# State-space chunks of a hybrid decoder trunk: sums between the rounds, read in their bank, lags shared with ACT, the skip term on GpSimd

## The chip, the cores and the metric

The kernel runs on one core of a Trainium2 chip. Its time is the device time of one execution in microseconds (us); three executions were timed before the change. One further execution was recorded by the profiler, and every row below is from it. TensorE (PE in the rows, PEld its weight loads) multiplies, VectorE is DVE, ScalarE is ACT, GpSimd is POOL and SyncE is SP; SP issues transfers.

## The reference

The program is a decoder trunk of two layers over 1024 tokens of width 1024. The change touches one part of the second layer's mixer, a diagonal state-space layer: 512 channels in 32 groups of 16, with 64 complex states a group.

```
ug = u.reshape(b, s, S5_GROUPS, S5_GROUP_CH)
bu_re = einsum('bsgc,gpc->bsgp', ug, bb_re)         # bu_im likewise
_, _, xr, xi = associative_scan(combine, (ar, ai, bu_re, bu_im), axis=1)   # x_t = a x_(t-1) + bu_t
y = einsum('bsgp,gcp->bsgc', xr, c_re) - einsum('bsgp,gcp->bsgc', xi, c_im)
y = y.reshape(b, s, S5_CH) + d_skip * u32
hg = gelu(y)
```

## The kernel before, in words

The sequence is cut into 128 chunks of `STEP` = 8 tokens, so that one matmul operand holds the 8 x 16 values of a chunk of one group on 128 partitions. Three things are needed. `q.into` turns a chunk into what it adds to the states (powers of the state matrix times B). `lags` holds for each of the 8 distances inside a chunk the 16x16 matrix C A^n B of a group; it is written on 16 partitions and then spread by eight transfers over the 128 partitions of `q.within`, each shifted by one token. And a scan over chunks carries the states along. `d_skip` enters as a diagonal added to the matrices of distance 0.

`s5_chunks` is one stage: it starts and ends with a barrier of all engines, and each engine's instructions run in the order in which they are written, held back only by semaphores. `NB` is 8 (one unit n is four groups), `P` 128, and a quarter k (0 to 3) is eight groups, thus units 2k and 2k+1. Every PSUM tile (`pa`, `pk`, `pb`, `pz`) has two banks, used in turn by even and odd n.

- TensorE: eight rounds; in each it transposes a unit of the powers (L2368, `pa`) and multiplies it with C (L2376, `pk`). ACT copies `pa` into `q.into` (L2414, tile `h` in the rows), VectorE copies `pk` into `lags` (L2432).
- VectorE then adds the skip term (L2436, made by L2427 from `d`), and SP issues the eight transfers (L2474, `h<-lags`). TensorE's first `outputs` waits for all of them (`spread`).
- `turn_u(n)` (L2324) transposes u, ACT copies it into `ut` (L2404), which lies in the memory of the powers (`bpow` in the rows; u itself is `gdn_t`). `sum_up(n)` (L2334) multiplies `q.into` with it into `pb`.
- VectorE, once a quarter: four copies of sums out of `pb` (L2448, L2449), a complex product with cosines and sines (L2110 to L2115 of `complex_times`: four products and two sums), two scans (L2457, L2458), and a second complex product. Then `scanned` is raised.
- `outputs(n)` (L2351 to L2353) adds three matmuls for each of four groups into `pk`, ACT applies gelu (L2410, into `s_t`), `turn_y` (L2361) transposes back, VectorE's `out` (L2440) writes y, in the memory of u.
- `keep_busy` (L131) issues matmuls whose results nobody reads.

In the order before, TensorE runs all rounds, then `turn_u` and `sum_up` from quarter to quarter, with the sums of quarter k+1 ahead of or beside the outputs of quarter k-1. Each `sum_up` of a later quarter waits for VectorE's copies (`s_copied`), each output for `scanned`. The next stage's work, `s5_glu` with its weights' transfers, starts behind the barrier.

Of the kernel before, what the change touches and what calls it, by code (L numbers as in the profile page):

```python
# [11 lines left out]
ALU = mybir.AluOpType  # L12
# [3 lines left out]
P = 128  # L16
# [2275 lines left out]
def s5_chunks(nc, c, t, j, q, bpow, u, scratch):  # L2292
# [3 lines left out]

    y = output_of(u)
    QP, NB = PAIRS // 4, S5_GROUPS // 4
    ut = bpow[:].rearrange("p a t s -> p (a t) s")
    with ExitStack() as ctx:  # L2300
# [8 lines left out]
                 "summed", "s_copied", "scanned", "y_made", "y_copied", "y_turned", "y_out", "vec_steps")  # L2309
        with stage(nc, *names) as (block, (b_turned, b_copied, multiplied, k_copied, spread, d_in, skip_ready, skipped, u_turned, u_copied,  # L2310
                                           summed, s_copied, scanned, y_made, y_copied, y_turned, y_out, vs)):
            def group(n, a):
                return 8 * (n // 2) + 2 * a + n % 2

            @block.tensor
            def _(pe):
                def turn_u(n):
                    if n == 0:
                        pe.wait_ge(b_copied, NB)
                        pe.wait_ge(multiplied, NB)  # L2320
                    if n >= 2:
                        pe.wait_ge(u_copied, n - 1)
                    for a in range(4):
                        last = pe.transpose(pa[:, n % 2, a * P:(a + 1) * P], u[:, 4 * n + a, :, :].rearrange("p s c -> p (s c)"), c.ident[:])  # L2324
                    last.then_inc(u_turned, 1)

                def sum_up(n):
                    pe.wait_ge(u_copied, n + 1)
                    if n >= 2:
                        pe.wait_ge(s_copied, n - 1)  # L2330
# [8 lines left out]
                def outputs(n):  # L2339
                    if n == 0:  # L2340
                        pe.wait_ge(spread, 16 * STEP)
                        pe.wait_ge(k_copied, NB)
# [21 lines left out]
                for n in range(NB):  # L2364
                    if n >= 2:
                        pe.wait_ge(b_copied, n - 1)
                    for a in range(4):
                        last = pe.transpose(pa[:, n % 2, a * P:(a + 1) * P], bpow[:, a % 2, 2 * n + a // 2, :], c.ident[:])  # L2368
                    last.then_inc(b_turned, 1)
                    if n >= 2:  # L2370
                        pe.wait_ge(k_copied, n - 1)
                    for a in range(4):
                        g = group(n, a)
                        half = slice((g % 2) * S5_STATE, (g % 2 + 1) * S5_STATE)
                        for part, cc in ((0, q.c_re), (1, q.c_nim)):
                            last = pe.matmul(pk[0:S5_GROUP, n % 2, a * P:(a + 1) * P],  # L2376
                                             bpow[half, part, g // 2, (STEP - 1) * S5_GROUP:STEP * S5_GROUP],
                                             cc[half, g // 2, 0:STEP, :], start=(part == 0), stop=(part == 1))
                    last.then_inc(multiplied, 1)
                for k in range(6):  # L2380
                    if k < 4:
                        turn_u(2 * k)
                        turn_u(2 * k + 1)
                    if k == 2:
                        keep_busy(pe, c, pz[:, 0], 24)
                    if 1 <= k <= 4:
                        sum_up(2 * k - 2)
                        sum_up(2 * k - 1)
                    if k >= 3:
                        outputs(2 * k - 6)  # L2390
                        outputs(2 * k - 5)
# [9 lines left out]
            def _(act):  # L2401
                def u_copy(n):
                    act.wait_ge(u_turned, n + 1)
                    act.activation(ut[:, 4 * n:4 * n + 4, :].rearrange("p g c -> p (g c)"), pa[:, n % 2, :], ACT.Copy).then_inc(u_copied, 1)  # L2404
# [16 lines left out]
            def _(dve):  # L2421
                step = Steps(dve, vs)
                for a in range(2):
                    dve.memset(x_re[:, a, :, 0:1], 0.0)
                    dve.memset(x_im[:, a, :, 0:1], 0.0)
                dve.wait_ge(d_in, 16)
                dve.tensor_tensor(skip, d[:].unsqueeze(2).to_broadcast([S5_GROUP, S5_GROUPS, S5_GROUP]),  # L2427
                                  c.ident[0:S5_GROUP, 0:S5_GROUP].unsqueeze(1).to_broadcast([S5_GROUP, S5_GROUPS, S5_GROUP]),
                                  ALU.mult).then_inc(skip_ready, 1)
                for n in range(NB):  # L2430
                    dve.wait_ge(multiplied, n + 1)
                    dve.tensor_copy(lags[:, 8 * (n // 2) + n % 2:8 * (n // 2) + 8:2],  # L2432
                                    pk[0:S5_GROUP, n % 2, :].rearrange("p (g s) -> p g s", g=4)).then_inc(k_copied, 1)
                dve.wait_ge(skip_ready, 1)
# [815 lines left out]
```

## Time and profile before

| | us |
|---|---|
| median of three timed executions | 3115.54 (3115.08 to 3117.53) |
| the profiled execution's own time | 3113.26 |
| its span, first to last instruction | 3111.7 |
| TensorE busy | 2926.2 (94%), mean granted clock 0.975 |
| VectorE, ACT, GpSimd busy | 1129.9 (36%), 668.1 (21%), 238.4 (8%) |

Three executions differ by 2.5 us. The shares are means over a program whose stages have different limits, so they say little of one stage of some 87 us. In it the reader looks at which engine waits for which, row by row. The granted clock is a share of TensorE's full speed: 1.00 is 2.4 GHz, 0.50 is 1.2 GHz.

### The profile page before, as it was taken

How to read it: one execution, taken by the hardware profiler on the slowest of the kernel's cores; microseconds unless marked ns; L12 is line 12 of the kernel's file. 1: busy time of each engine (PE TensorE's matmuls, PEld its weight loads, DVE VectorE, ACT ScalarE, POOL GpSimd, SP SyncE). 2: the span in 40 equal slices, each digit the busy share in tenths (PEclk: the TensorE clock that was granted, in tenths of full speed). 3: DMA queues.
4: the chain of work that ended last, by engine and by line, in shares of the span. 5: the costliest groups of instructions: out<-in, count | busy, mean ns of one | idle time of the engine just before them, and what ended most of it. 6: DMA issues, size and time to landing. Idle time of an engine off the chain costs nothing. (4 is left out here: it accounts for less than half of the span.)

```text
span 3111.7 us, 33248 instructions
## 1 busy us (share of the span) xinstructions
PE 2926.2 (94%) x12773; PEld 1588.0 (51%) x12774; DVE 1129.9 (36%) x2472; ACT 668.1 (21%) x1278; POOL 238.4 (8%) x344
## 2 busy tenths in 40 slices
PE   7999999999999999988989999878999999999798
PEld 5544555555544444434467744477555444444343
DVE  2585355534300000005464635565563000000152
ACT  3310355531110101003321224322211101010130
POOL 0000000001000000002000000144110000000110
PEclk9999999999999999999999999889999999999899
DMA  4000791031599999966020110000416999999631
GB/s 159 27 27 0 285 407 65 1 118 57 186 422 410 413 412 413 395 274 230 34 65 1 29 56 27 1 2 29 158 57 263 410 419 413 411 413 400 264 136 41
DMA packets 138551, 617.26 MB, mean 198 GB/s; under 512 B 25188, under 2 KB 31748, under 8 KB 121992
## 3 DMA queue, kind: packets, MB, share of 16 engines
q1 hardware_dynamic: 111848, 529.08, 43.0%
q0 software_dynamic: 23168, 82.85, 6.9%
q10 hardware_dynamic: 3376, 3.19, 0.3%
q8 instruction: 103, 1.69, 0.2%
q14 instruction: 56, 0.46, 0.0%
HBM read 508.00 MB, written 105.91 MB: 197 GB/s over the span
## 5 line engine op out<-in xcount | busy, mean ns | idle before, releaser
L1944 PE MATMUL acc<-wg,xt 128*128 128x512 f32 x512 | 223.5, 597 | 0.0
L2598 PE MATMUL acc<-xt,work 128*128 128x512 f32 x384 | 166.9, 593 | 0.0
L667 PE MATMUL acc<-h,xt 128*128 128x512 f32 x384 | 165.2, 592 | 0.0
L1944 PEld LDWEIGHTS acc<-wg,xt 128*128 128x128 f32 x512 | 97.7, 192 | 120.2 <-issue 120.2
L305 PE MATMUL scores<-qkt 65*128 65x512 f32 (+7 forms) x384 | 146.0, 489 | 0.4 <-DVE qkt L446 0.4
L452 DVE TENSOR_REDUCE nmax<-scores 128x1 f32<-128x256 f32 (+7 forms) x128 | 96.8, 756 | 74.0 <-PE scores L307 70.7
L1664 PE MATMUL py<-place 128*64 128x512 f32 (+1 forms) x352 | 120.2, 595 | 1.0 <-DVE place L1744 1.0
L1664 PE MATMUL pu<-place 128*128 128x512 f32 (+1 forms) x320 | 119.8, 593 | 0.0
L667 PEld LDWEIGHTS acc<-h,xt 128*128 128x128 f32 x384 | 72.9, 190 | 91.1 <-issue 90.9
L2598 PEld LDWEIGHTS acc<-xt,work 128*128 128x128 f32 x384 | 72.0, 190 | 86.1 <-issue 86.1
L1177 PE MATMUL acc<-place 128*128 128x512 f32 x256 | 112.7, 594 | 1.1 <-PEq L64 1.1
L1750 DVE COPY work<-py 128x512 f32<-128x512 f32 x25 | 17.3, 692 | 241.1 <-PE py L1664 241.1
L1750 DVE COPY place<-py 128x512 f32<-128x512 f32 x25 | 17.3, 692 | 241.1 <-PE py L1664 241.1
L1664 PE MATMUL pg<-place 128*128 128x512 f32 (+1 forms) x288 | 101.6, 596 | 0.0
L399 ACT ACTIVATE probs<-scores,nmax 128x256 f32<-128x256 f32 (+7 forms) x128 | 94.3, 736 | 8.0 <-DVE nmax L452 6.6
L763 ACT ACTIVATE place<-acc 128x256 f32<-128x256 f32 (+4 forms) x88 | 39.8, 473 | 242.5 <-PE acc L667 242.4
L2272 PE MATMUL acc<-s_t,xt 128*128 128x260 f32 (+1 forms) x256 | 85.6, 496 | 1.1 <-PEq L64 1.1
L1731 ACT ACTIVATE work<-pg 128x512 f32<-128x512 f32 x25 | 14.9, 597 | 326.5 <-PE pg L1664 326.5
L1731 ACT ACTIVATE place<-pg 128x512 f32<-128x512 f32 x25 | 14.9, 597 | 326.5 <-PE pg L1664 326.5
L1783 DVE TENSOR_TENSOR work<-work,pu 128x512 f32<-128x512 f32 x25 | 17.2, 688 | 183.8 <-PE pu L1664 183.8
L1783 DVE TENSOR_TENSOR place<-place,pu 128x512 f32<-128x512 f32 x25 | 17.2, 688 | 183.8 <-PE pu L1664 183.8
L305 PEld LDWEIGHTS scores<-qkt 65*128 65x128 f32 (+1 forms) x384 | 62.8, 190 | 33.1 <-issue 32.7
(647 smaller groups left out, 5193.6 us busy)
## 6 DMA issues: line engine op xcount, KB each, us to landing
own<-in_moe_w_gate_dram SPq DMA_DIRECT2D x22, 2048.0 KB, 18.9
place<-in_moe_w_down_dram SPq DMA_DIRECT2D x22, 2048.0 KB, 19.7
place<-in_moe_w_up_dram SPq DMA_DIRECT2D x20, 2048.0 KB, 19.6
slots_out<-zeros SPq DMA_DIRECT2D x4, 9216.0 KB, 63.0
place<-in_moe_w_gate_dram SPq DMA_DIRECT2D x18, 2048.0 KB, 23.4
own<-in_moe_w_up_dram SPq DMA_DIRECT2D x16, 2048.0 KB, 17.7
own<-in_moe_w_down_dram SPq DMA_DIRECT2D x10, 2048.0 KB, 22.5
xt<-in_moe_w_gate_dram SPq DMA_DIRECT2D x9, 2048.0 KB, 24.1
```

What stands on the lines that cost most here:

```text
L305: pe.matmul(bank(n, u)[:, a * SLAB:a * SLAB + w], qkt[0:kind(p).rows, p % 2, u, 0, i * P:(i + 1) * P], qkt[0:kind(p).rows, p % 2, u, 1, a ...
L399: act.activation(probs[:, u, n % 2, 0:(i + 1) * P], bank(n, u), ACT.Exp, bias=nmax[:, n % 2, u:u + 1], accum_out=total[:, (n // NT) % 2, i ...
L452: dve.tensor_reduce(nmax[:, n % 2, u:u + 1], bank(n, u), AX.X, ALU.max, negate=True).then_inc(maxed, 1)
L667: last = pe.matmul(acc[:, n % 4, 0:width], xs[:, k, tile_of(i)], weights[:, k, cols], start=(k == 0), stop=(k == k_of - 1))
L763: last = act.activation(place, part, ACT.Copy)
L1177: last = pe.matmul(acc[:, n, :], columns(k, i), slabs[n][:, k, :], start=(k == 0), stop=(k == KD - 1))
L1664: last = pe.matmul(out[part], lhs[:, k, part], weights_of(kind, q)[:, k, cols], start=(k == 0), stop=(k == k_last), skip_group_check=True)
L1750: dve.tensor_copy(y[:, n % 2, SLAB:D], py[:, SLAB:D]).then_inc(y_dve, 1)
L1783: dve.tensor_tensor(hid, gate, pu[:], ALU.mult).then_inc(hidden, 1)
L1944: last = pe.matmul(acc[:, u % 4, :], xt[:, k, i * P:(i + 1) * P], wg[:, k, n * SLAB:(n + 1) * SLAB], start=(k == 0), stop=(k == KD - 1))
L2272: ins = pe.matmul(acc[:, n % 4, 0:width], xt[:, k, at], slab[:, k, 0:width], start=(k == 0), stop=(k == KD - 1))
L2598: last = pe.matmul(acc[:, n % 4, :], slabs[m // 4 % 2][:, k, (m % 4) * P:(m % 4 + 1) * P], xt[:, k, half * SLAB:(half + 1) * SLAB], start= ...
```

## The change

1. TensorE does four rounds, then `turn_u(0)` and `turn_u(1)`, then four more rounds, with `sum_up(0)` behind the fifth and `sum_up(1)` behind the sixth. The banks of `pa` are handed on in one list of slots. Then come the other six `turn_u`, the sums of quarter 1, ten `keep_busy` matmuls, and a loop over the quarters in which the sums of quarter k+2 stand between the outputs and the `turn_y` of quarter k.
2. ACT copies units 4 to 7 of the lags, each behind its copy for `q.into`; VectorE copies units 0 to 3 only.
3. The skip term is made and added on GpSimd, which waits for both engines' copies.
4. VectorE no longer copies the sums. The four products read them in `pb`; a new semaphore `sums_read` is raised behind the complex product, and `sum_up(n)` waits for it from n = 2 on.

TensorE between the rounds and the first outputs, before (`L2376` matrices, `L2324` u, `L2334` sums, `L131` fillers, `L2351` the first output):

```order
L2376 MATMUL pk<-c_nim,bpow 16x128
L2324 MATMUL pa<-ident,gdn_t 128x128 x16
L2334 MATMUL pb<-bpow,h 64x128 x16
L2324 MATMUL pa<-ident,gdn_t 128x128 x8
L131 MATMUL pz<-ident 128x128 x24
L2334 MATMUL pb<-bpow,h 64x128 x16
L2324 MATMUL pa<-ident,gdn_t 128x128 x8
L2334 MATMUL pb<-bpow,h 64x128 x16
L2351 MATMUL pk<-bpow,h 128x128
```

The same place after (`L2353` matrices, `L2361` u, `L2372` sums, `L2390` the first output):

```order
L2353 MATMUL pk<-c_nim,bpow 16x128
L2361 MATMUL pa<-ident,gdn_t 128x128 x24
L2372 MATMUL pb<-bpow,h 64x128 x16
L131 MATMUL pz<-ident 128x128 x10
L2390 MATMUL pk<-bpow,h 128x128
```

Two `turn_u` and two sums have left this place for the rounds, and the third quarter's sums for the place behind the first outputs.

TensorE behind the first quarter's outputs, after (before, `L2361`, now `L2400`, stood directly behind the outputs and the sums behind it):

```order
L2392 MATMUL pk<-x_im,c_nim 128x128
L2372 MATMUL pb<-bpow,h 64x128 x16
L2400 MATMUL pz<-ident,s_t 128x128 x8
L2390 MATMUL pk<-bpow,h 128x128
L2391 MATMUL pk<-x_re,c_re 128x128
```

The sums now stand ahead of `turn_y`, for which VectorE's `out` waits.

VectorE from the end of a quarter to the next one's products, quarter 0 to 1 before:

```order
L2115 TENSOR_TENSOR x_im<-s_t 128x4x128
L2461 ISA
L2448 COPY s_re<-pb 128x2x128
L2449 COPY s_im<-pb 128x2x128
L2448 COPY s_re<-pb 128x2x128
L2449 COPY s_im<-pb 128x2x128
L2110 TENSOR_TENSOR s_t<-cosn,s_re 128x512
L2111 TENSOR_TENSOR s_t<-sinn,s_im 128x512
```

and quarter 1 to 2 after (`L2490` is `out`, `L2507` and `L2500` raise semaphores):

```order
L2115 TENSOR_TENSOR x_im<-s_t 128x4x128
L2507 ISA
L2490 COPY gdn_t<-pz 128x4x8x16 x2
L2110 TENSOR_TENSOR s_t<-cosn,pb 128x512
L2111 TENSOR_TENSOR s_t<-sinn,pb 128x512
```

The four copies are gone, and the products take `pb`, the bank.

```diff
+            slots = [("b", n) for n in range(4)] + [("u", 0), ("u", 1)] + [("b", n) for n in range(4, NB)] + [("u", n) for n in range(2, NB)]
+
+            def before_in_slot(what, n):
+                at = slots.index((what, n)) - 2
+                if at < 0:
+                    return None
+                what, n = slots[at]
+                return (b_copied if what == "b" else u_copied), n + 1
+
+            def two_pairs(x):
+                return x.rearrange("p (a b) n -> p a b n", a=2)
+
+            def summed_of(part):
+                return pb[:, :, 2 * P * part:2 * P * (part + 1)].rearrange("p a (b n) -> p a b n", b=2)
...
+                def claim(what, n):
+                    before = before_in_slot(what, n)
+                    if before:
+                        pe.wait_ge(*before)
+
+                def turn_b(n):
+                    claim("b", n)
+                    for a in range(4):
+                        last = pe.transpose(pa[:, n % 2, a * P:(a + 1) * P], bpow[:, a % 2, 2 * n + a // 2, :], c.ident[:])
+                    last.then_inc(b_turned, 1)
+
+                def matrices(n):
+                    if n >= 6:
+                        pe.wait_ge(k_copied_act, n - 5)
+                    elif n >= 2:
+                        pe.wait_ge(k_copied, n - 1)
...
+                    last.then_inc(multiplied, 1)
...
                 def turn_u(n):
-                    if n == 0:
-                        pe.wait_ge(b_copied, NB)
-                        pe.wait_ge(multiplied, NB)
-                    if n >= 2:
-                        pe.wait_ge(u_copied, n - 1)
+                    claim("u", n)
...
                     pe.wait_ge(u_copied, n + 1)
+                    pe.wait_ge(b_copied, n + 1)
                     if n >= 2:
-                        pe.wait_ge(s_copied, n - 1)
+                        pe.wait_ge(sums_read, n // 2)
...
-                        pe.wait_ge(k_copied, NB)
+                        pe.wait_ge(k_copied, 4)
+                        pe.wait_ge(k_copied_act, NB - 4)
...
-                for n in range(NB):
-                    if n >= 2:
...
-                for k in range(6):
-                    if k < 4:
-                        turn_u(2 * k)
-                        turn_u(2 * k + 1)
-                    if k == 2:
-                        keep_busy(pe, c, pz[:, 0], 24)
-                    if 1 <= k <= 4:
-                        sum_up(2 * k - 2)
-                        sum_up(2 * k - 1)
-                    if k >= 3:
-                        outputs(2 * k - 6)
-                        outputs(2 * k - 5)
-                        turn_y(2 * k - 6)
-                        turn_y(2 * k - 5)
-                keep_busy(pe, c, pa[:, 0], 10)
-                outputs(NB - 2)
-                outputs(NB - 1)
-                turn_y(NB - 2)
-                turn_y(NB - 1)
+                for n in range(4):
+                    turn_b(n)
+                    matrices(n)
+                turn_u(0)
+                turn_u(1)
+                for n in range(4, NB):
+                    turn_b(n)
+                    matrices(n)
+                    if n < 6:
+                        sum_up(n - 4)
+                for n in range(2, NB):
+                    turn_u(n)
+                sum_up(2)
+                sum_up(3)
+                keep_busy(pe, c, pz[:, 0], 10)
+                for k in range(4):
+                    outputs(2 * k)
+                    outputs(2 * k + 1)
+                    if k < 2:
+                        sum_up(2 * k + 4)
+                        sum_up(2 * k + 5)
+                    turn_y(2 * k)
+                    turn_y(2 * k + 1)
+
+            @block.gpsimd
+            def _(pool):
+                groups = [S5_GROUP, S5_GROUPS, S5_GROUP]
+                pool.wait_ge(d_in, 16)
+                pool.tensor_tensor(skip, d[:].unsqueeze(2).to_broadcast(groups), c.ident[0:S5_GROUP, 0:S5_GROUP].unsqueeze(1).to_broadcast(groups),
+                                   ALU.mult).then_inc(skip_ready, 1)
+                pool.wait_ge(skip_ready, 1)
+                pool.wait_ge(k_copied, 4)
+                pool.wait_ge(k_copied_act, NB - 4)
+                pool.tensor_tensor(lags[:, :, 0:S5_GROUP], lags[:, :, 0:S5_GROUP], skip, ALU.add).then_inc(skipped, 1)
+
...
                 def u_copy(n):
                     act.wait_ge(u_turned, n + 1)
+                    if n < 2:
+                        act.wait_ge(multiplied, 2 * n + 2)
+                    else:
+                        act.wait_ge(multiplied, NB)
                     act.activation(ut[:, 4 * n:4 * n + 4, :].rearrange("p g c -> p (g c)"), pa[:, n % 2, :], ACT.Copy).then_inc(u_copied, 1)
...
-                for n in range(NB):
-                    act.wait_ge(b_turned, n + 1)
-                    act.activation(q.into[:, 2 * n:2 * n + 2, :, :].rearrange("p t r s -> p (t r s)"), pa[:, n % 2, :], ACT.Copy).then_inc(b_copied, 1)
-                for n in range(NB):
+                for n in range(4):
+                    b_copy(n)
+                u_copy(0)
+                u_copy(1)
+                for n in range(4, NB):
+                    b_copy(n)
+                    act.wait_ge(multiplied, n + 1)
+                    act.activation(*lags_of(n), ACT.Copy).then_inc(k_copied_act, 1)
+                for n in range(2, NB):
                     u_copy(n)
...
-                dve.wait_ge(d_in, 16)
-                dve.tensor_tensor(skip, d[:].unsqueeze(2).to_broadcast([S5_GROUP, S5_GROUPS, S5_GROUP]),
-                                  c.ident[0:S5_GROUP, 0:S5_GROUP].unsqueeze(1).to_broadcast([S5_GROUP, S5_GROUPS, S5_GROUP]),
-                                  ALU.mult).then_inc(skip_ready, 1)
-                for n in range(NB):
+                for n in range(4):
                     dve.wait_ge(multiplied, n + 1)
-                    dve.tensor_copy(lags[:, 8 * (n // 2) + n % 2:8 * (n // 2) + 8:2],
-                                    pk[0:S5_GROUP, n % 2, :].rearrange("p (g s) -> p g s", g=4)).then_inc(k_copied, 1)
-                dve.wait_ge(skip_ready, 1)
-                dve.wait_ge(k_copied, NB)
-                dve.tensor_tensor(lags[:, :, 0:S5_GROUP], lags[:, :, 0:S5_GROUP], skip, ALU.add).then_inc(skipped, 1)
+                    dve.tensor_copy(*lags_of(n)).then_inc(k_copied, 1)
 
...
-                    for n in (2 * k, 2 * k + 1):
-                        two = slice(2 * (n % 2), 2 * (n % 2) + 2)
-                        dve.wait_ge(summed, n + 1)
-                        dve.tensor_copy(s_re[:, v, two, 1:], pb[:, n % 2, 0:2 * P].rearrange("p (t n) -> p t n", t=2))
-                        dve.tensor_copy(s_im[:, v, two, 1:], pb[:, n % 2, 2 * P:4 * P].rearrange("p (t n) -> p t n", t=2)).then_inc(s_copied, 1)
-                    dve.wait_ge(s_copied, 2 * k + 2)
+                    four = [two_pairs(x) for x in t4]
+                    turned = [two_pairs(x) for x in (x_re[:, v, :, 1:], x_im[:, v, :, 1:], q.cosn[:, part, :], q.sinn[:, part, :])]
+                    dve.wait_ge(summed, 2 * k + 2)
                     if k >= 2:
                         dve.wait_ge(y_made, 2 * k - 2)
-                    complex_times(dve, step, x_re[:, v, :, 1:], x_im[:, v, :, 1:], q.cosn[:, part, :], q.sinn[:, part, :],
-                                  s_re[:, v, :, 1:], s_im[:, v, :, 1:], t4, conj=True)
+                    complex_times(dve, step, *turned, summed_of(0), summed_of(1), four, conj=True)
+                    dve.engine_nop().then_inc(sums_read, 1)
```

## Rows read from the trace of the kernel before

**Rows 1.** Windows, after a half-clock return: us, busy time of engines, PEclk, DMA share, GB/s
```profile
1747.00:1750.30 3.30, 3.06 (x30) 3.09 (x32) 3.26 (x7) 0.00 (x0) 0.00 (x0) 0.50 0.00 0
```
**Rows 2.** TensorE in order of time: start, us, line, operation, operands, count, idle before
```profile
1706.20 0.66 PE L2368 MATMUL pa<-ident,bpow 128*128 128x128 f32 x4
...
1716.16 1.06 PE L2324 MATMUL pa<-ident,gdn_t 128*128 128x128 f32 x8
1717.47 1.14 PE L2324 MATMUL pa<-ident,gdn_t 128*128 128x128 f32 x8 [0.25 <-ACT bpow L2404]
1718.54 1.97 PE L2334 MATMUL pb<-bpow,h 128*64 128x128 f32 x32
...
1721.37 5.52 PE L131 MATMUL pz<-ident 128*128 128x128 f32 x48
...
1732.37 2.89 PE L2334 MATMUL pb<-bpow,h 128*64 128x128 f32 x32 [2.55 <-DVE s_im L2449]
1735.19 0.80 PE L2351 MATMUL pk<-bpow,h 128*128 128x128 f32 x2
...
1744.29 1.41 PE L2361 MATMUL pz<-ident,s_t 128*128 128x128 f32 x8
1747.24 3.44 PE L2334 MATMUL pb<-bpow,h 128*64 128x128 f32 x32 [1.54 <-DVE s_im L2449]
1750.62 0.49 PE L2351 MATMUL pk<-bpow,h 128*128 128x128 f32 x2
...
1759.07 1.41 PE L2361 MATMUL pz<-ident,s_t 128*128 128x128 f32 x8
...
1772.77 0.49 PE L2351 MATMUL pk<-bpow,h 128*128 128x128 f32 x2 [0.45 <-DVEq L2461]
...
1783.68 1.07 PE L2525 MATMUL pt<-ident,gdn_t 128*128 128x128 f32 x8 [1.05 <-PEq L64]
```
**Rows 3.** VectorE in order of time, same columns
```profile
1716.83 0.68 DVE L2436 TENSOR_TENSOR lags<-lags,s_t 16x512 f32<-16x512 f32 x1
...
1721.35 0.69 DVE L2110 TENSOR_TENSOR s_t<-cosn,s_re 128x512 f32<-128x512 f32 x1
...
1731.47 0.42 DVE L2448 COPY s_re<-pb 128x256 f32<-128x256 f32 x1
...
1744.99 1.45 DVE L2440 COPY gdn_t<-pz 128x512 f32<-128x512 f32 x2 [1.99 <-PE pz L2361]
1746.35 0.41 DVE L2448 COPY s_re<-pb 128x256 f32<-128x256 f32 x1
...
1747.80 0.69 DVE L2110 TENSOR_TENSOR s_t<-cosn,s_re 128x512 f32<-128x512 f32 x1
```
**Rows 4.** The eight spreading transfers: line L2474, then the last one's us to landing
```profile
L2474 SPq DMA_DIRECT2D h<-lags x8: 622/1753/3300, 1717.5 to 1730.3; - x8
...
h<-lags SPq DMA_DIRECT2D x1, 32.0 KB, 3.9
```
**Rows 5.** Single lines: ns min/median/max of one, first and last start
```profile
L2414 ACT ACTIVATE h<-pa x8: 597/597/597, 1697.2 to 1714.2; 128x512 f32<-128x512 f32 x8
...
L3127 POOL TENSOR_TENSOR gbz<-gbz,gains x8: 1267/1272/1281, 2172.7 to 2198.8; 128x512 f32<-128x512 f32 x8
...
L1783 DVE TENSOR_TENSOR work<-work,pu x25: 686/689/689, 2385.8 to 2919.0; 128x512 f32<-128x512 f32 x25
```
**Rows 6.** TensorE's return after a long wait, and a window from there on
```profile
1404.78 3.68 PE L1916 MATMUL acc<-ident,normed 128*128 128x128 f32 x16 [15.69 <-DMA normed<-in_p_dram]
...
1404.80:1408.90 4.10, 3.65 (x16) 3.25 (x16) 0.00 (x0) 2.20 (x4) 2.95 (x4) 0.50 1.02 410
```
**Rows 7.** VectorE and GpSimd beside each other in a later stage, in order of time
```profile
2011.60 0.41 DVE L2940 TENSOR_TENSOR below<-work,bank 64x256 f32<-64x256 f32 x1
2011.94 1.69 DVE L2944 TENSOR_TENSOR tri<-work,firsts 64x256 f32<-64x256 f32 x2
...
2012.45 0.90 POOL L3045 TENSOR_TENSOR bt<-nat,levels 128x256 f32<-128x256 f32 x1
```

More of the change, by code:

```diff
@@ L2308, in s5_chunks @@
         names = ("b_turned", "b_copied", "multiplied", "k_copied", "spread", "d_in", "skip_ready", "skipped", "u_turned", "u_copied",
-                 "summed", "s_copied", "scanned", "y_made", "y_copied", "y_turned", "y_out", "vec_steps")
+                 "summed", "sums_read", "k_copied_act", "scanned", "y_made", "y_copied", "y_turned", "y_out", "vec_steps")
         with stage(nc, *names) as (block, (b_turned, b_copied, multiplied, k_copied, spread, d_in, skip_ready, skipped, u_turned, u_copied,
-                                           summed, s_copied, scanned, y_made, y_copied, y_turned, y_out, vs)):
+                                           summed, sums_read, k_copied_act, scanned, y_made, y_copied, y_turned, y_out, vs)):
@@ L2315, in _ @@
+            def summed_of(part):
+                return pb[:, :, 2 * P * part:2 * P * (part + 1)].rearrange("p a (b n) -> p a b n", b=2)
             @block.tensor
             def _(pe):
-                def turn_u(n):
-                    if n == 0:
-                        pe.wait_ge(b_copied, NB)
-                        pe.wait_ge(multiplied, NB)
-                    if n >= 2:
-                        pe.wait_ge(u_copied, n - 1)
+                def claim(what, n):
[12 more added lines that the diff above has]
+                        pe.wait_ge(k_copied, n - 1)
+                    for a in range(4):
+                        g = group(n, a)
+                        half = slice((g % 2) * S5_STATE, (g % 2 + 1) * S5_STATE)
+                        for part, cc in ((0, q.c_re), (1, q.c_nim)):
+                            last = pe.matmul(pk[0:S5_GROUP, n % 2, a * P:(a + 1) * P],
+                                             bpow[half, part, g // 2, (STEP - 1) * S5_GROUP:STEP * S5_GROUP],
+                                             cc[half, g // 2, 0:STEP, :], start=(part == 0), stop=(part == 1))
+                    last.then_inc(multiplied, 1)
+                def turn_u(n):
+                    claim("u", n)
@@ L2362, in turn_y @@
                     last.then_inc(y_turned, 1)
-                for n in range(NB):
-                    if n >= 2:
[L2366 to L2379, printed above, removed]
@@ L2400, in _, with lags_of, outputs_of, b_copy @@
+            def lags_of(n):
+                return lags[:, 8 * (n // 2) + n % 2:8 * (n // 2) + 8:2], pk[0:S5_GROUP, n % 2, :].rearrange("p (g s) -> p g s", g=4)
+            def outputs_of(n):
+                return (y.rearrange("p s (g c) -> p g s c", c=S5_GROUP)[:, 8 * (n // 2) + n % 2:8 * (n // 2) + 8:2],
+                        pz[:, n % 2, :].rearrange("p (g s c) -> p g s c", g=4, s=STEP))
             @block.scalar
             def _(act):
+                def b_copy(n):
+                    act.wait_ge(b_turned, n + 1)
+                    act.activation(q.into[:, 2 * n:2 * n + 2, :, :].rearrange("p t r s -> p (t r s)"), pa[:, n % 2, :], ACT.Copy).then_inc(b_copied, 1)
@@ L2434, in _ @@
-                dve.wait_ge(skip_ready, 1)
-                dve.wait_ge(k_copied, NB)
-                dve.tensor_tensor(lags[:, :, 0:S5_GROUP], lags[:, :, 0:S5_GROUP], skip, ALU.add).then_inc(skipped, 1)
+                for n in range(4):
+                    dve.wait_ge(multiplied, n + 1)
+                    dve.tensor_copy(*lags_of(n)).then_inc(k_copied, 1)
                 def out(n):
                     dve.wait_ge(y_turned, n + 1)
-                    dve.tensor_copy(y.rearrange("p s (g c) -> p g s c", c=S5_GROUP)[:, 8 * (n // 2) + n % 2:8 * (n // 2) + 8:2],
-                                    pz[:, n % 2, :].rearrange("p (g s c) -> p g s c", g=4, s=STEP)).then_inc(y_out, 1)
+                    dve.tensor_copy(*outputs_of(n)).then_inc(y_out, 1)
```

## The prediction

> **What bounds the kernel now.** I read the windows first, then TensorE's rows in order of time, then VectorE's, and last the transfers. The stage that changes runs from about 1697 us (ACT's first copy [rows 5]) to 1783.68, where the next stage's first matmul stands [rows 2]: 87 of 3111.7 us. The next stage waits for all engines; its own transfers are issued only then, so what this stage gains or loses passes to the end one for one. Four stretches follow each other in it.
>
> First the eight rounds (`turn_b` and matrices), bound by TensorE alone: the fifth round starts at 1706.20 and the block after the eighth at 1716.16 [rows 2], so four rounds take 9.96 us. Second, copies of u, the first sums, and the first quarter of the scan on VectorE from 1721.35; a quarter's arithmetic takes 10.12 us, to 1731.47 [rows 3]. TensorE has no work here that pays: 24 filler matmuls (5.52 us), then 2.55 us of waiting before 1732.37 [rows 2]. Third, two alternating engines: TensorE makes two groups of outputs (8.45 us from 1750.62 to 1759.07 at full clock, 9.10 from 1735.19 to 1744.29, where the first matmuls took 0.80 us instead of 0.49 [rows 2]), VectorE moves them out (1.36 us for two, 1744.99 to 1746.35), copies the next sums (1.45 us to 1747.80) and computes the next quarter [rows 3]. Fourth a tail: from the last outputs' start, 1772.77, to the next stage, 10.91 us [rows 2].
>
> A second path runs beside it: after VectorE's skip addition (1716.83 plus 0.68) SP issues eight transfers that spread the lags over 128 partitions. The first is issued at 1717.5, the last at 1730.3, and that one lands 3.9 us later [rows 4]: 16.7 us, to 1734.2. `outputs(0)` needs all of them. It started at 1735.19, directly behind the sums. So in the old order this path was hidden with only 1.0 us to spare. That is the row on which my forecast turns.
>
> **The change part by part.**
>
> Two copies of u and two sums move in between the rounds. Two `turn_u` and the wait for ACT's copy behind them cost 1.31 us (1716.16 to 1717.47), two `sum_up` 1.97 us [rows 2]. Nothing hides them, since TensorE is the bound there; the lags are complete 3.3 us later, the last round ending at about 1719.4.
>
> The last four lag copies go to ACT. ACT's 128x512 copies take 0.60 us; VectorE's copies of lags 0.68, as its addition of the same size does [rows 3, 5], the form is new on ACT, and I take 0.60; between 0.5 and 0.9 bounds it. ACT has the time, as one copy of 0.60 us in a round of 2.5 shows. Worth -0.1 us on the spread's path.
>
> The skip addition goes to GpSimd. It has no such row; on 16 partitions with 512 elements the nearest rows are 1.27 us for a GpSimd operation of 512 elements a partition [rows 5] and VectorE's own 0.68 us [rows 3] as the floor. I take 1.2, so +0.5. It adds a wait too: the addition reads SBUF while VectorE is in its scan. At 2012.45 a GpSimd operation and two VectorE ones of 64x256 with both inputs in SBUF ran together: VectorE's took 1.69 us for two, when 64x256 on the same engine with one operand in a bank took 0.41 [rows 7]. Whoever comes second waits. If GpSimd comes second, behind a scan, the price is up to 1.2 us; if VectorE does, up to 1.3, in a stretch where it then waits for sums anyway. I take +0.1.
>
> The Trainium skill says this as a rule (SBUF — State Buffer, Who interferes with whom): a VectorE instruction with both inputs in SBUF and a GpSimd one that reads SBUF exclude each other for a whole instruction. By that rule the trace agrees, and the copies' new home speaks against the change where VectorE's operands are in SBUF, not where one is in a bank.
>
> Sum of the spread's path: 1717.5 + 3.3 - 0.1 + 0.5 + 0.1 = 1721.3 for the first issue, + 16.7 = 1738.0 for the last landing; from 1737.4 to 1739.4 by the bounds. `outputs(0)` starts at 1738.0, 2.8 us later than before, with nothing to cover it.
>
> TensorE's part of that wait: after the last round, six more `turn_u` at 1.31 us a pair (3.9), sums 2 and 3 (1.97), and ten fillers instead of 24 (10/24 of 5.52 = 2.3) end at 1727.6. It then idles 10.4 us. At 1404.78 it came back from 15.69 us of idling and the clock stayed at half (1.2 GHz) for another 4.2 us [rows 6]. At half clock sums take 3.44 us instead of 1.97 [rows 1, 2]; so 4.2 us do the work of 2.4, and the first two outputs take 8.45 + 1.8 = 10.25 us, to 1748.2.
>
> VectorE starts its first quarter at 1714.6 (1706.20 + 1.31 + two rounds of 2.5 + 1.97) and ends it at 1724.7; the second starts behind sums 2 and 3, at 1725.4, and ends at 1735.5. There it waits: its next work needs outputs 0 and 1, which haven't begun. What this order saves on VectorE reaches nobody.
>
> Reading the sums in their bank takes away four copies, 1.45 us a quarter [rows 3]. The four products now have one operand in a bank: 0.689 us at 128x512 [rows 5] as against 0.69 for those in SBUF [rows 3]; the same, so 0, and +0.3 us a product as the upper bound (nearest: none dearer in the rows), never below 0. The gain applies to quarters 2 and 3, on the path: 2.9 us. In quarters 0 and 1 it is hidden.
>
> But `sum_up` now waits for `sums_read`, and VectorE's wait for `turn_y(0)` comes behind sums 4 and 5, which stand ahead of it on TensorE: +1.97 us between outputs 1 and quarter 2. In the old order these ran beside VectorE's work.
>
> The chain from 1738.0: outputs 0, 1 to 1748.2; sums 4, 5 to 1750.2; first `out` 0.70 us after `turn_y` starts and 1.36 for two, 1752.2; quarter 2 to 1762.3. TensorE meanwhile: `turn_y` 1.4, outputs 2, 3 8.45, sums 6, 7 1.97, to 1762.0; out 2 and 3 behind `turn_y`, 2.06 more, 1764.0; quarter 3 to 1774.2; outputs 6 start 0.1 later, 1774.3; tail 10.91: 1785.2. Before it was 1783.7: +1.5. TensorE is done with `turn_y(5)` at about 1773.2 and idles 1.1 us, and after 1.54 us at 1747.24 the clock fell to half for 3.1 us [rows 1, 2]; that would cost 1.3, I count a third: +0.4. Sum: +1.9 us. On the profiled execution's own 3113.3 us that is 3115.2; the three timed runs have their median 2.3 us higher, and since times are compared I forecast **3117.4 us**.
>
> **Rivals.**
>
> (a) The spread is quicker than 16.7 us, or not on the path. For it: its packets may have waited for traffic which the trace doesn't separate. Against: no other issue stands beside these eight in that stretch. Each microsecond less is one gained, down to where TensorE's 1727.6 binds: then outputs 0 start 10.4 us earlier at full clock, -12.2 + 1.9 = about -10: 3105 us. A spread of 12 us gives 3113.
>
> (b) The change's reads in the bank don't do what they say: a product with an operand in four pieces in two banks costs 0.3 us more than one in SBUF. For quarters 2 and 3 that is 8 x 0.3 = 2.4 us: 3119.8.
>
> (c) Slower: the clock. After 10.4 us of idling TensorE works at half clock not for 4.2 us but through outputs 0 and 1: 8.45 x 3.44/1.97 = 14.8 us, 4.5 more than in my sum; with GpSimd behind a scan (+1.1) and the half clock at the tail too (+0.9) it ends at +8.4, 3123.8. Outputs 0 and 1 taking over 14.6 us alone would decide it. Against: after 15.69 us of idling it took 4.2 us, and from 1750.62 on, 3.4 us after a return, the outputs ran at their full pace [rows 2, 6].
>
> **Chances.** Forecast 0.62, (a) 0.14, (b) 0.10, (c) 0.14. A change under 0.2%, 6.2 us, can't be told from none here. Of (a) less than half passes -6.2 us: faster 0.06. Of (c) half passes +6.2: slower 0.07. Same 0.87. Forecast's own range is 3115 to 3120; with (a) to a spread of 11 us and (b), (c) in part the range is 3111.5 to 3122.5.
>
> **What would show it.** Right: the eighth round ends near 1719.4; the addition on GpSimd about 1.2 us long; first spread issued near 1721.3; TensorE idle some 10 us, released by the spread's last landing; the clock half ahead of and behind that; products from the bank at 0.69 us; VectorE idle over 10 us behind quarter 1; the stage ending 1 to 3 us later. Wrong: the wait ahead of the first outputs ends with something other than the spread, or it is under 5 us; then the stage would end before 1780 and the time be under 3112.

## The result: 0.5% slower

The changed kernel's five executions have a median of 3130.56 us (3129.66 to 3136.92), against 3115.36 us for the kernel before; the ratio is 1.0053, with a 95% interval of 1.0043 to 1.0064. My forecast was 3117.4, in a range of 3111.5 to 3122.5. The profiled execution took 3136.92 us and is the slowest of its five. In it the stage of the state-space chunks lasts from 1699.88 to 1801.49, 101.6 us; before it was 87.2. These 14.4 us are near the 15.2 by which the medians differ. The profiled execution is 23.7 us longer than its counterpart; the other 9.3 lie outside the stage, 3.4 of them ahead of it (it starts at 1699.88 instead of 1696.50) and 5.9 behind it. So the program's time can differ between two executions by microseconds in which the stage has no part.

TensorE in order of time in the changed kernel, from the rounds' start to the next stage, with the same columns as [rows 2]; `L2390` is an output's first matmul, `L2372` sums, `L2400` `turn_y`, `L131` fillers:

```profile
1699.88 0.63 PE L2341 MATMUL pa<-ident,bpow 128*128 128x128 f32 x4 [0.94 <-PEq L64]
...
1722.71 1.09 PE L2361 MATMUL pa<-ident,gdn_t 128*128 128x128 f32 x8
...
1728.37 2.50 PE L131 MATMUL pz<-ident 128*128 128x128 f32 x20
1741.94 0.80 PE L2390 MATMUL pk<-bpow,h 128*128 128x128 f32 x2 [11.07 <-DMA h<-lags]
...
1756.93 3.68 PE L2372 MATMUL pb<-bpow,h 128*64 128x128 f32 x32
1760.54 1.23 PE L2400 MATMUL pz<-ident,s_t 128*128 128x128 f32 x8
1761.61 0.39 PE L2390 MATMUL pk<-bpow,h 128*128 128x128 f32 x2
...
1784.04 0.49 PE L2390 MATMUL pk<-bpow,h 128*128 128x128 f32 x2 [1.43 <-DVEq L2507]
...
1801.49 6.43 PE L2571 MATMUL pt<-ident,gdn_t 128*128 128x128 f32 x32 [1.05 <-PEq L64]
```

The first outputs wait 11.07 us, and the profile names the spread (`DMA h<-lags`) as what ended the wait. Outputs 0 and 1 then take 14.99 us (1741.94 to 1756.93) where before they took 9.10 [rows 2], and the last two with the tail behind them 17.45 us (1784.04 to 1801.49) where before they took 10.91. The number and form of the matmuls are the same. The windows, with the columns of [rows 1] (the number behind the five engines is the granted clock), say why:

```profile
1733.60:1741.90 8.30, 0.00 (x0) 0.00 (x0) 5.37 (x8) 0.00 (x0) 0.00 (x0) 0.50 0.62 68
1741.90:1756.90 15.00, 14.96 (x48) 11.40 (x48) 0.00 (x0) 0.60 (x1) 0.00 (x0) 0.50 0.00 1
1756.90:1760.80 3.90, 3.90 (x34) 3.54 (x34) 0.00 (x0) 0.60 (x1) 0.00 (x0) 0.50 0.00 0
1760.90:1784.70 23.80, 22.27 (x156) 17.60 (x155) 22.95 (x34) 2.39 (x4) 0.00 (x0) 1.00 0.00 1
1784.80:1801.30 16.50, 15.64 (x54) 11.83 (x52) 1.83 (x3) 1.19 (x2) 0.00 (x0) 0.50 0.00 0
```

TensorE is at half clock for the end of the wait, for both outputs, and for the sums behind them; and again from 0.8 us into the last outputs to the end of the stage, though it had waited only 1.43 us there. In the kernel before, the last outputs ran at full clock, and around the first ones the clock was half for little more than 3 us:

```profile
1733.50:1735.20 1.70, 1.70 (x18) 1.37 (x15) 1.70 (x4) 0.00 (x0) 0.00 (x0) 0.50 0.08 13
1735.20:1736.50 1.30, 1.30 (x5) 1.07 (x5) 1.26 (x3) 0.00 (x0) 0.00 (x0) 0.50 0.00 0
1736.50:1744.00 7.50, 7.50 (x44) 5.81 (x44) 6.40 (x9) 0.60 (x1) 0.00 (x0) 0.99 0.00 0
```

The first of these windows holds the sums behind the wait of 2.55 us, the others outputs 0 and 1: the clock came back 1.4 us into them.

The rest of the stage went about as its trace of before promised. VectorE, GpSimd and SP in the changed kernel:

```profile
1719.16 0.68 DVE L2112 TENSOR_TENSOR s_t<-cosn,pb 128x512 f32<-128x512 f32 x1
...
1724.20 1.60 DVE L2110 TENSOR_TENSOR s_t<-cosn,s_re 128x512 f32<-128x512 f32 x1
...
1738.35 0.69 DVE L2115 TENSOR_TENSOR x_im<-s_t 128x512 f32<-128x512 f32 x1
1761.37 1.29 DVE L2490 COPY gdn_t<-pz 128x512 f32<-128x512 f32 x2 [22.33 <-PE pz L2400]
1762.57 0.68 DVE L2110 TENSOR_TENSOR s_t<-cosn,pb 128x512 f32<-128x512 f32 x1
...
1702.12 1.05 POOL L2431 TENSOR_TENSOR s_t<-d,ident 16x512 f32<-16x512 f32 x1 [115.88 <-DMA d<-in_s_d_dram]
1723.57 1.67 POOL L2436 TENSOR_TENSOR lags<-lags,s_t 16x512 f32<-16x512 f32 x1 [20.41 <-ACT lags L2472]
...
1725.27 14.26 SPq L2520 DMA_DIRECT2D h<-lags  x8
```

A product with an operand in the bank takes 0.68 us, as in SBUF. The addition on GpSimd takes 1.67 us; the same addition with VectorE idle takes 1.26 in a run below. The VectorE product that starts beside it takes 1.60 us instead of 0.69. So each was longer by their meeting. (The row at 1702.12, 1.05 us, makes the skip term; it has other operands.) VectorE ends quarter 1 at 1739.0 and then stands still for 22.33 us.

To compare stages, I count from their first matmul:

| us from the stage's start | before | changed |
|---|---|---|
| first spread issued | 21.0 | 25.4 |
| outputs 0 | 38.7 | 42.1 |
| outputs 2 | 54.1 | 61.7 |
| outputs 4 | 63.8 | 72.9 |
| outputs 6 | 76.3 | 84.2 |
| next stage | 87.2 | 101.6 |

### The profile page after: what moved, and what is told of

The parts are those of the page before. It is cut to its first block and busy times, and to the rows that moved or that the text cites. A ratio compares the mean times of both kernels' runs of the same rounds, so it can differ in the third digit from the quotient of the medians.

```text
span 3135.4 us, 33151 instructions
## 1 busy us (share of the span) xinstructions
PE 2943.7 (94%) x12725; PEld 1599.1 (51%) x12726; DVE 1120.7 (36%) x2450; ACT 671.4 (21%) x1282; POOL 240.7 (8%) x346
## 5 line engine op out<-in xcount | busy, mean ns | idle before, releaser
L667 PEld LDWEIGHTS acc<-h,xt 128*128 128x128 f32 x384 | 72.9, 190 | 91.1 <-issue 90.9
L1664 PE MATMUL pg<-place 128*128 128x512 f32 (+1 forms) x288 | 101.6, 596 | 0.0
```

The source lines that it names most:

```text
L667: last = pe.matmul(acc[:, n % 4, 0:width], xs[:, k, tile_of(i)], weights[:, k, cols], start=(k == 0), stop=(k == k_of - 1))
L1664: last = pe.matmul(out[part], lhs[:, k, part], weights_of(kind, q)[:, k, cols], start=(k == 0), stop=(k == k_last), skip_group_check=True)
```

## The experiments

The kernel before ran beside all of them, with medians of 3114.83, 3114.89 and 3115.37 us in the three groups. Its own times are spread: of 66 executions 18 lie between 3119 and 3125, one took 3137 and one 3531. The profiles vary outside the stage too: from the stage's end to the program's end they last from 1327.4 to 1334.6 us. So a stage's gain and the median's need not be the same to some microseconds. A ratio is the time against the kernel before, with a 95% interval in brackets.

**Fillers over the long wait.**

```diff
-                keep_busy(pe, c, pz[:, 0], 10)
+                keep_busy(pe, c, pz[:, 0], 56)
```

> The changed kernel with 56 instead of 10 filler matmuls ahead of the first outputs. In the changed kernel's trace TensorE waits 11.07 us there for the spread, the clock is half from before the end of this wait until 18.9 us after it, and outputs 0 and 1 take 15.0 us (8.45 at full clock), the sums behind them 3.6 (1.9). Theory A (the half clock behind the long wait is the cost, not the wait): the fillers cover about 10.6 us of the wait, outputs 0 and 1 take 8.5 to 9.2 us, sums 2.0, and the time falls by 8 us against the changed kernel's 3130.6, to about 3122.5. Rival B (the late landing is the cost): the landing stays where it is, the fillers change less than 2 us, 3129 to 3131. If both outputs 6, 7 stay at half clock as in the changed kernel, the tail is still 17.5 us.

3125.21 us (3119.99 to 3128.5), ratio 1.0020 (0.9998 to 1.0042). The stage took 92.5 us instead of 101.6. TensorE in it:

```profile
1728.28 12.77 PE L131 MATMUL pz<-ident 128*128 128x128 f32 x112
1741.81 0.49 PE L2390 MATMUL pk<-bpow,h 128*128 128x128 f32 x2 [0.77 <-DMA h<-lags]
...
1750.27 1.97 PE L2372 MATMUL pb<-bpow,h 128*64 128x128 f32 x32
```

The spread lands at the same point of the stage (42.0 us), and the outputs take 8.46 us at a clock of 1.00. So work that computes nothing gives back 9.1 us of the stage; of the median it gives back 5.4, less than the 8 expected. For these 9.1 us Rival B, the wait in itself as the cost, is out.

**Fillers ahead of the last outputs.**

```diff
                 for k in range(4):
+                    if k == 3:
+                        keep_busy(pe, c, pa[:, 0], 6)
                     outputs(2 * k)
```

> The changed kernel with 6 filler matmuls ahead of the last quarter's outputs, where it waits 1.43 us and where the kernel before had 10. Theory A: outputs 6 and 7 run at full clock, the tail from outputs 6 to the next stage falls from 17.45 to 10.9 us, and the next stage's first transposes from 6.4 to 4.7 us: 3130.6 - 8 = about 3122.5. Rival B: the half clock in the tail came from something else (a window of the clock that the short wait does not decide): no change, 3129 to 3131. Rival C: the fillers only lengthen the path, +0.3 us.

3127.74 us (3126.69 to 3129.01), ratio 1.0035 (1.0019 to 1.0051). The tail is 10.92 us instead of 17.45, the stage 94.8. The first stretch at half clock is unchanged (outputs 0 and 1 take 14.99 us). The median fell by 2.8 us, less than the stage's 6.8 and the 8 expected, so the stage's gain is shown by the profile and only in part by the times.

**Both** edits together.

> The changed kernel with both fillers, 56 ahead of the first outputs and 6 ahead of the last. Theory A: both half-clock stretches of the stage go; what is left against the kernel before is the start of the first outputs 3.4 us later and the quarter's copies saved (about 3.5 us): the same time as before, 3114 to 3117. Rival B: 3125 or more, the loss is in the waits themselves.

3117.47 us (3112.83 to 3121.7), ratio 1.0007 (0.9997 to 1.0018); the stage takes 86.4 us and no part of it is at half clock. 15.2 us of 101.6 were the clock. What is left of the change is a gain of 0.8 us against a stage that before held some half clock itself [rows 2]: outputs 0 start 3.1 us later than before, and from there to the stage's end it takes 3.9 us less.

**The spread in halves.** Groups 0 to 15 are spread behind the fourth round, the others behind the last; the addition on GpSimd is halved likewise, and outputs 4 wait for the second half.

```diff
+                    if n == NB // 2:
+                        pe.wait_ge(spread_late, 16 * STEP)
...
+                for part, landed in enumerate((spread, spread_late)):
+                    some = slice(part * S5_GROUPS // 2, (part + 1) * S5_GROUPS // 2)
+                    sp.wait_ge(skipped, part + 1)
                     for s in range(STEP):
```

> The changed kernel with the spread in two halves: groups 0 to 15 (units 0 to 3, complete after the fourth round) get their skip term and their eight transfers at once, groups 16 to 31 theirs behind the last round; outputs 0 wait only for the first half, outputs 4 for the second. If the late landing is what makes TensorE wait (and with that the clock fall), the first half lands before 1727 on the changed kernel's time axis, outputs 0 start right behind the ten fillers, at about 1731 instead of 1741.9, at full clock: 11 us of waiting and 7.6 us of half clock go, of which VectorE's chain takes some back: 3130.6 - 17 = about 3113, and 3107 if the tail's clock stays full as well. Rival: many small transfers issued in the midst of the rounds slow one another or the halves take longer than 8.4 us each; then outputs 0 wait again, and the time stays above 3122.

3111.21 us (3108.98 to 3113.35), ratio 0.9985 (0.9976 to 0.9995). Outputs 0 start at 30.8 us of the stage, behind the fillers and with no wait, and the stage takes 80.1 us. The last outputs, behind a wait of 1.41 us, are at half clock again, from some 3 us into them, and the tail is 15.66 us. The halved addition on GpSimd took 0.72 us alone and 1.20 beside VectorE's scan.

**Fillers behind the wait.**

```diff
-                keep_busy(pe, c, pz[:, 0], 10)
+                pe.wait_ge(spread, 16 * STEP)
+                keep_busy(pe, c, pz[:, 0], 14)
```

> The changed kernel with 14 fillers BEHIND the wait for the spread instead of 10 ahead of it. TensorE then idles 13.5 us instead of 11.07, so the clock is half when the spread lands. Theory A2 (what comes first behind the wait decides: dense 128x128 matmuls bring the clock back within some 4 us, as the transposes at 1404.78 and the sums of the stage do, while outputs never end a half-clock stretch): the fillers start at half clock, take about 5 us, and outputs 0 and 1 take 8.5 to 9.5 us instead of 15.0; with the 5 us paid for fillers the time is 1 to 3 us below the changed kernel, 3128 to 3130, with the tail as there. Rival B2 (the length of the half-clock stretch follows from the length of the wait, here 27 us for 11): the outputs still take 15 us, and the time is 5 us or more above, 3135.

3131.75 us (3127.1 to 3132.01), ratio 1.0050 (1.0034 to 1.0067). TensorE's rows, and two windows of the same kernel:

```profile
1739.27 5.70 PE L131 MATMUL pz<-ident 128*128 128x128 f32 x28 [13.48 <-DMA h<-lags]
1744.81 0.39 PE L2390 MATMUL pk<-bpow,h 128*128 128x128 f32 x2
...
1753.16 1.97 PE L2372 MATMUL pb<-bpow,h 128*64 128x128 f32 x32
```

```profile
1739.20:1744.00 4.80, 4.73 (x22) 4.74 (x23) 0.00 (x0) 0.00 (x0) 0.00 (x0) 0.50 0.00 0
1744.20:1753.10 8.90, 8.90 (x55) 7.02 (x54) 0.00 (x0) 0.60 (x1) 0.00 (x0) 1.00 0.01 2
```

This run tells the mechanism, though its time is no better: 3128 to 3130 were expected, and the stage is only 2.4 us shorter than the changed kernel's, at 99.2. The wait was longer still (13.48 us) and the clock half when it ended. Dense 128x128 matmuls came first, and 4.8 us later the clock was full; the outputs took 8.35 us. In the changed kernel outputs came first, and 15.0 us later the clock was still half. So the length of the wait alone does not set how long the half clock lasts; what TensorE does behind it counts.

**All rounds first**, the interleaving undone (the `slots`, ACT's order and TensorE's):

```diff
-                for n in range(4):
+                for n in range(NB):
                     turn_b(n)
                     matrices(n)
                 turn_u(0)
                 turn_u(1)
-                for n in range(4, NB):
-                    turn_b(n)
-                    matrices(n)
-                    if n < 6:
-                        sum_up(n - 4)
+                sum_up(0)
+                sum_up(1)
```

> The changed kernel with its first part undone: all eight rounds first, then u 0, 1 and sums 0, 1, then the rest as changed (lags shared with ACT, skip term on GpSimd, sums read in their bank). The lags are complete 3.3 us earlier, the first spread is issued 3.5 to 4 us earlier, TensorE waits about 7 us for its landing. If the interleaving is what makes the spread late: outputs 0 start at 38.7 us of the stage as in the kernel before, but the wait of 7 us still brings the half clock: outputs 0 and 1 about 15 us; 3 to 4 us less than the changed kernel, 3126 to 3128. If the interleaving was harmless: 3130 to 3132.

3128.96 us (3128.16 to 3130.66), ratio 1.0043 (1.0026 to 1.0059). Outputs 0 start at 38.3 us, 3.7 earlier than in the changed kernel and 0.4 earlier than before the change. That is the interleaving's price. But TensorE waits 7.12 us ahead of them, and they take 14.99 us. A start as early as before does not help: in the old order sums stood between the wait and the outputs, here nothing does. (The old order's wait was shorter too, 2.55 us against 7.12. The run with fillers behind the wait is the one that tells the two apart.)

**The bank alone.** The kernel before, with only the copies removed and `sums_read` in place of `s_copied`:

```diff
-                        dve.tensor_copy(s_re[:, v, two, 1:], pb[:, n % 2, 0:2 * P].rearrange("p (t n) -> p t n", t=2))
...
+                    complex_times(dve, step, *turned, *sums, four, conj=True)
+                    dve.engine_nop().then_inc(sums_read, 1)
```

> The kernel before with one part of the change alone: the products read the sums in their bank, the copies are gone, sum_up waits for sums_read. Each quarter is 1.45 us shorter on VectorE, products stay at 0.69 us. Sums of the next quarter start later than before (they waited for the copies, now for the whole product of 3.9 us), which lengthens TensorE's waits at 1732 and 1747. Theory A: the later sums put the waits at 5 us and 4 us and lower the clock, the gain is eaten: 3112 to 3122. Rival: 1.45 us in each of three quarters on the path are gained, 3110 to 3112.

3122.08 us (3120.13 to 3131.63), ratio 1.0029 (1.0019 to 1.0039). The stage takes 92.4 us, 5.2 more than before:

```profile
1737.10 3.68 PE L2334 MATMUL pb<-bpow,h 128*64 128x128 f32 x32 [4.86 <-DVEq L2452]
...
1755.61 3.45 PE L2334 MATMUL pb<-bpow,h 128*64 128x128 f32 x32 [4.65 <-DVEq L2452]
```

The waits for VectorE were 2.55 and 1.54 us [rows 2]. Now they are 4.86 and 4.65, because `sums_read` is raised only when the whole complex product is done. Removing four cheap copies lengthens the hold on the bank by more than they cost, where the next sums stand right behind it. Another 0.8 us came from the clock, which was half for all of the first of these sums (3.68 us instead of 2.89). The last two operations of the product don't read the bank, and they fill 1.3 us ahead of the sums; a semaphore raised before them was not tried.

**ACT and GpSimd alone**, in the kernel before (lags 4 to 7 as in the change's diff):

```diff
+                pool.wait_ge(k_copied, 4)
+                pool.wait_ge(k_copied_act, NB - 4)
+                pool.tensor_tensor(lags[:, :, 0:S5_GROUP], lags[:, :, 0:S5_GROUP], skip, ALU.add).then_inc(skipped, 1)
...
+                    if n >= 4:
+                        act.wait_ge(multiplied, n + 1)
+                        act.activation(*lags_of(n), ACT.Copy).then_inc(k_copied_act, 1)
```

> The kernel BEFORE with one part of the change alone: lags 4 to 7 copied by ACT, the skip term made and added on GpSimd. The addition takes 1.05 us undisturbed instead of 0.68 (more if VectorE reads two SBUF operands beside it), the copy 0.59 instead of 0.68; the first spread is issued 0.3 to 0.6 us later. In the order of before there is 1.0 us to spare ahead of outputs 0. Theory A: covered, stage 87 to 88 us, 3113 to 3117. Rival: the addition collides with VectorE as in the changed kernel (1.67 us) and the spread becomes late by 0.3 us or more with half-clock outputs behind it: 3120 or more.

3120.54 us (3114.28 to 3126.3), ratio 1.0008 (0.9996 to 1.0019): no difference clear of the noise. The stage took 90.6 us in the profile, where 87 to 88 were expected. VectorE was idle beside the addition:

```profile
1717.57 1.26 POOL L2415 TENSOR_TENSOR lags<-lags,s_t 16x512 f32<-16x512 f32 x1 [16.99 <-ACT lags L2434]
```

It took 1.26 us, and outputs 0 start at 38.8 us of the stage, 0.1 later than before: covered. Outputs 6 start at 74.8 us, 1.5 earlier than in the profile of before, since the sums of [rows 2] at 1747.24 ran at full clock this time (1.97 us). Then the profiled execution lost 4.9 us in the tail:

```profile
1772.00:1774.80 2.80, 2.76 (x16) 2.16 (x17) 1.25 (x2) 0.00 (x0) 0.00 (x0) 1.00 0.02 6
1775.00:1784.80 9.80, 9.80 (x33) 7.38 (x32) 0.00 (x0) 0.60 (x1) 0.00 (x0) 0.50 0.00 0
```

There TensorE had waited 0.43 us, as before the change (0.45). The clock fell all the same, 2.8 us into the outputs. Its ten times lie in two groups, near 3114 and from 3118 up, as the kernel before has some near 3120. That this place parts the groups, by a clock that falls in some executions and not in others, is a guess: one execution of the ten was profiled.

**The kernel before without its fillers in the tail.**

```diff
-                keep_busy(pe, c, pa[:, 0], 10)
```

> The kernel BEFORE without its ten fillers ahead of the last outputs. TensorE then waits about 2.85 us there instead of 0.45. Theory A (a wait of 1.4 us or more right ahead of outputs puts them at half clock and outputs do not end it): outputs 6 and 7 run at half clock, the tail is 15 to 18 us instead of 10.9, the stage 92 to 94 us instead of 87.2, the time 3119 to 3122. Rival B (the changed kernel's tail fell for a reason of its own order, such as the long wait before): the tail stays at 11 to 12 us, 3113 to 3116.

3123.60 us (3119.55 to 3125.35), ratio 1.0021 (1.0012 to 1.0031).

```profile
1771.54 0.79 PE L2351 MATMUL pk<-bpow,h 128*128 128x128 f32 x2 [2.67 <-DVEq L2460]
...
1789.54 6.80 PE L2524 MATMUL pt<-ident,gdn_t 128*128 128x128 f32 x32 [1.05 <-PEq L64]
```

The tail is 18.0 us. In the same trace a wait of 1.54 us, with sums behind it, was followed by outputs at full clock. The loss needs nothing of the changed kernel's order: a wait of 2.67 us with outputs behind it was enough, in the profile and by the times, all ten of which lie at 3119.5 or above.

**A version that beats both**: the spread in halves, no fillers ahead of the first outputs, six ahead of the last. Beside the split's edit:

```diff
-                keep_busy(pe, c, pz[:, 0], 10)
                 for k in range(4):
+                    if k == 3:
+                        keep_busy(pe, c, pa[:, 0], 6)
                     outputs(2 * k)
```

> The changed kernel with the spread in halves, no fillers ahead of the first outputs (with the split spread nothing is waited for there, and the ten fillers stood on the path for 2.3 us) and 6 fillers ahead of the last outputs. Theory A: outputs 0 start 2.3 us earlier than with the split spread alone, the tail runs at full clock (10.9 instead of 15.7 us): the stage takes 80.1 - 2.3 - 4.8 = 73 us, 14 less than the kernel before: 3102 to 3104. Rival: without the fillers the clock falls at the start of the outputs, then they take 15 us and the time is 3110 or more.

> The kernel with the split spread, no fillers ahead of the first outputs and six ahead of the last, once more in five rounds, since its seven times lie between 3099 and 3108 (one aside): the stage takes 73.3 us, 13.9 less than before. If the stage decides, the mean is about 3101 to 3103; if the clock elsewhere in the program takes some of it back (the earlier medians), 3105 to 3108.

First group: 3106.5 us (six executions, 3099.4 to 3108.13; a seventh took 3932.82 and is left out), ratio 0.9962 (0.9947 to 0.9977), a few microseconds above the 3102 to 3104 expected. Second: 3099.63 us (3099.09 to 3108.65), ratio 0.9951 (0.9936 to 0.9967). TensorE in the second:

```profile
1726.24 0.46 PE L2392 MATMUL pk<-bpow,h 128*128 128x128 f32 x2
...
1759.92 0.49 PE L2392 MATMUL pk<-bpow,h 128*128 128x128 f32 x2
...
1770.83 1.06 PE L2581 MATMUL pt<-ident,gdn_t 128*128 128x128 f32 x8 [1.05 <-PEq L64]
```

The stage takes 73.3 us in both profiles, 13.9 less than before and 28.3 less than the changed kernel. So of these 28.3 us 15.2 were the clock, by the run with both fillers, and 13.1 came from the earlier first half of the spread and the missing fillers. The times lie near 3100 or near 3107. The two profiles, 3105.38 and 3099.69, have the same stage; their difference lies ahead of it (2.3 us) and behind it (3.3). What makes it there stays open.

## Why the prediction was wrong, point by point

- Right: the wait ahead of the first outputs, released by the spread's last landing; 11.07 us against 10.4 forecast. The rounds' cost, 3.2 us (3.3 forecast), the spread's own 16.7 us, products from the bank at no extra price, VectorE's idling behind quarter 1.
- Right in kind, too small: GpSimd's addition. I took 1.2 + 0.1 us, it took 1.67. Alone it takes 1.26, so 1.2 was near and the meeting with VectorE cost 0.4, not 0.1. With the rest the first spread was issued 4.35 us later in the stage instead of 3.8, and outputs 0 started 3.4 us later instead of 2.8. Half a microsecond of the error.
- The step that failed is "so 4.2 us do the work of 2.4, and the first two outputs take 8.45 + 1.8 = 10.25 us". They took 14.99. I had taken the clock's return from the row at 1404.78, where 128x128 matmuls with `ident` follow the wait [rows 6], and what half clock costs from the sums at 1747.24 [rows 1, 2]. Behind this wait stand outputs. The run with fillers behind the wait shows that the return belongs to what follows: 4.8 us with dense matmuls, over 15 with outputs. 4.7 us of the error, and 1.6 more for the sums behind them (3.61 us from 1756.93 to 1760.54), for which I had reckoned 1.97 at full clock.
- The same mistake stands in the tail, "I count a third: +0.4". The tail lost 6.5 us. The row I priced it from, 1747.24, had sums behind its wait and 3.1 us at half clock; here outputs follow, and the clock was half for 16.7 us to the stage's end. 6.1 us of the error. The run without tail fillers repeats it in the kernel before.
- The sum: 0.6 + 4.7 + 1.6 + 6.1 = 13.0 us, less 0.6 by which quarters 2 and 3 with their copies came out shorter than I had reckoned: 12.4 against 12.5 measured (14.4 in the stage, 1.9 forecast).
- Rival (c) named what happened, the half clock through outputs 0 and 1, but not why, and was given 0.14. My argument against it, the outputs' full pace 3.4 us after a return, was the same row with sums ahead of the outputs. Rival (c) also priced outputs 0 and 1 rightly (14.8), but the tail at 1.3 us; with it the time would have been 3123.8, still 6.8 us short. Rival (b) is refuted by the products at 0.68 us. Rival (a) did not come true, since the spread took 16.7 us and was on the path. Its reckoning of what the landing holds up is borne out by the split spread: with the landing off the path, outputs 0 start 11.2 us earlier in the stage (10.4 reckoned).
- What I missed in the change itself: "reading the sums in their bank ... never below 0". Taken alone it costs 5.2 us in the old order, most of it through the longer hold on the bank. In the new order this hold is covered, since the sums stand far behind.

## What to carry to other kernels

When a reorder takes work out of a place where TensorE waits, price the wait by the instructions that come behind it at half clock, and not by its own length alone. For the clock's return use only a row where the same instructions follow the wait. Before moving work ahead of a producer that is long and hidden (here eight transfers of 16.7 us with 1.0 us to spare), split it so that its first half starts earlier. And a copy that frees a bank early can be worth more than the time it takes.

## What the runs showed of the hardware

- Outputs are three matmuls a group, two of them with 64 rows; TensorE is busy in the profile for 14.96 of 15.00 us. Where they stood right behind a wait and the clock was half, it was still half when they were over: in the changed kernel (27 us at half), in the run with fillers in the tail alone, in the run with all rounds first, and in seven tails. It came back 3 to 4 us into the sums, or 3 to 6 us into the next stage's transposes.
- They do not always hold it down. In the kernel before, the bank-alone run, the ACT-and-GpSimd run and the run without tail fillers, sums stood between the wait and outputs 0, and the half clock ended 0.9 to 1.4 us into the outputs, 4.1 to 4.6 us behind the wait. Why outputs on their own don't bring the clock back as the 128x128 fillers do was not tried and stays open.
- The clock fell as little as 2.8 us into outputs behind a wait of only 0.43 us in one profile, and not in the kernel before's with 0.45. In the five tails behind a wait of 1.4 us it fell before they began in one, and 3.0 us into them at the latest. Six fillers in place of the wait kept it up in the four profiles that had them. No run here tells when exactly it falls.
- GpSimd's addition of 16x512: 1.26 us with VectorE idle, 1.67 beside its scan and products; VectorE's product beside it 1.60 instead of 0.69.
